# A two-layer hybrid mixer and MoE network on one core: the even layer's conditioning, gates and mLSTM moved between the outputs of its projection

## The reference, cut to what matters

```
mod = split(silu(c) @ ada_w[l] + ada_b[l], 6)          # for both layers; 0 shift, 1 scale, 2 gate of the mixer, 3..5 of the MoE
u = h * (1 + mod[1]) + mod[0]
p = u @ even_w_in                                      # 8 groups of 512 columns, and 16 gate columns
mLSTM, per head and direction (forward, backward):
    b = cumsum(log_sigmoid(f)); m = running max;       # from the gate columns
    s = (q k^T) * exp(log_d - m);  h = (s v) / max(|sum s|, exp(-m))
y_a = head_norm(h_fwd + h_bwd) * sigmoid(o)
y_b = HGRN(q, i, f_fwd, f_bwd) normed * silu(g)
y = [y_a, y_b] @ even_w_out;  h = layer_norm(ALPHA * h + mod[2] * y)
```

## Time and profile before

| | us |
|---|---|
| median of 3 runs (2417.41 to 2431.5) | 2421.47 |
| the profiled execution, its own time | 2445.92 |
| its span | 2444.1 |
| PE busy / DVE busy / ACT busy / POOL busy in the span | 1965.7 / 848.3 / 236.9 / 648.3 |
| mean granted TensorE clock | 0.892 |

### The profile page before, as it was taken

The page is one execution under the profiler, slowest core; times in us unless marked ns, Lnnn a source line. Parts: engine busy times, 40 slices in busy tenths (PEclk is TensorE's granted clock), DMA queues, the critical chain, the costliest instruction groups (busy, mean ns, idle before and its releaser), DMA issues. The chain is left out here.

```text
span 2444.1 us, 31822 instructions
## 1 busy us (share of the span) xinstructions
PE 1965.7 (80%) x10720; PEld 1014.9 (42%) x10721; DVE 848.3 (35%) x1752; ACT 236.9 (10%) x517; POOL 648.3 (27%) x935
## 2 busy tenths in 40 slices
PE   4795759945767998899999976859777988787795
PEld 0342523323445454455555433324454544344342
DVE  0004630068546232232332254644353222222224
ACT  1102110122020000000000011011110000000001
POOL 0000000000002555466565400000005554444440
PEclk8895679977887999899999987979878999999998
DMA  9400047300216899999899476130248999999944
GB/s 386 175 1 1 0 176 295 117 1 1 91 46 255 330 410 412 415 392 361 347 393 383 179 309 234 52 137 35 91 164 334 416 420 422 422 422 420 419 193 189
DMA packets 99975, 601.67 MB, mean 246 GB/s; under 512 B 23200, under 2 KB 23435, under 8 KB 40444
## 3 DMA queue, kind: packets, MB, share of 16 engines
q1 hardware_dynamic: 66012, 516.78, 51.7%
q0 software_dynamic: 33888, 83.86, 9.2%
HBM read 590.50 MB, written 51.92 MB: 263 GB/s over the span
## 5 line engine op out<-in xcount | busy, mean ns | idle before, releaser
L1600 PE MATMUL bank<-moe_w,blk_xT 128*64 128x256 f32 x5632 | 678.8, 396 | 2.7 <-issue 2.7
L1600 PEld LDWEIGHTS bank<-moe_w,blk_xT 128*64 128x64 f32 x5632 | 404.2, 142 | 220.0 <-issue 32.7
L1611 PE MATMUL bank<-moe_w,xt 128*64 128x512 f32 x1408 | 332.1, 592 | 1.5 <-DVE xt L1688 1.5
L1527 POOL DMA_INDIRECT ada_rows<-v_tokens,blk_gidx x264 | 272.5, 1032 | 140.0 <-issue 134.9
L1676 DVE STREAM_TRANSPOSE blk_xT<-ada_rows 128x512 f32<-128x512 f32 x132 | 93.9, 711 | 526.7 <-PE bank L1600 497.9
L451 PE MATMUL bank<-w_in_ring,xt 128*128 128x512 f32 x544 | 244.0, 609 | 12.6 <-DMA w_in_ring<-in_odd_w_in 9.7
L1543 POOL DMA_INDIRECT y_rows<-xt,blk_sidx x176 | 179.9, 1022 | 92.4 <-issue 55.0
L451 PEld LDWEIGHTS bank<-w_in_ring,xt 128*128 128x128 f32 x544 | 105.1, 195 | 148.7 <-issue 138.6
L1611 PEld LDWEIGHTS bank<-moe_w,xt 128*64 128x64 f32 x1408 | 100.9, 137 | 127.5 <-issue 100.5
L1659 ACT ACTIVATE xt<-bank 128x128 f32<-128x128 f32 x174 | 48.4, 278 | 1062.5 <-PE bank L1600 1062.5
L1695 DVE COPY xt<-bank 128x512 f32<-128x512 f32 x176 | 121.4, 690 | 75.0 <-PE bank L1611 73.2
(11 more groups left out here) (385 smaller groups left out, 1690.8 us busy)
## 6 DMA issues: line engine op xcount, KB each, us to landing
moe_w<-in_experts SPq DMA_DIRECT2D x128, 3072.0 KB
ada_ring<-in_ada_w SPq DMA_DIRECT2D x12, 2048.0 KB, 16.8
w_out<-in_ada_w POOLq DMA_DIRECT2D x12, 2048.0 KB, 8.2
moe_w<-y_rows SPq DMA_DIRECT2D x24, 1024.0 KB, 19.8
w_in_ring<-in_even_w_in SPq DMA_DIRECT2D x8, 2048.0 KB, 12.7
w_in_ring<-in_odd_w_in SPq DMA_DIRECT2D x7, 2048.0 KB, 20.9
ada_rows<-v_tokens,blk_gidx POOLq DMA_INDIRECT x264
w_out<-in_even_w_out SPq DMA_DIRECT2D x1, 4096.0 KB, 12.6
```

Source lines behind the costliest of these rows:

```text
L1527: pool.indirect_dma_start(came[q][:, u], None, v_quarters, bass.IndirectOffsetOnAxis(ap=gidx[q][:, u:u + 1], axis=0), bounds_check=4 * n_t ...
L1600: last = nc.tensor.matmul(g.bank[1][64 * h:64 * h + 64, 0:HID], xT[:, k], w[:, s, (2 * k + h) * HID:(2 * k + h + 1) * HID], start=k == 0, ...
L1611: last = nc.tensor.matmul(g.bank[3][64 * h:64 * h + 64, :], hT[:, 64 * m:64 * m + 64], w[:, s, at:at + 512], start=m == 0, stop=m == 1)
```

## The change

The stages 1 to 8 of the list above become three.

- `start_stage`: SP loads `c_cols`, then the four pieces of group 0 of layer 0 alone (shift and scale of the mixer), then the tables, the biases of both layers, and the tokens last. PE, ACT and DVE work the one group to its columns.
- `modulate_stage` without the gate rows (`rows` is None), with the loads of two groups of `even_w_in`; the ring has two places in place of three. The gate rows move to the start of `norm_stage` "h" (`mod_rows` on PE, four copies on ACT).
- `projection_stage` over all eight groups, 32 outputs, with `EvenSide` as its side. Two banks are left for the outputs (`BANKS = 2`; it was eight and six). The side has the other six: one for conditioning, one for the running maximum and the transposes of `mix`, two for scores (two key tiles at a time, so the scores are made in two halves), two for values. One more slot (`TAIL`) follows the last output.

What stands in the slots: gate columns in slot 1, their ACT and DVE parts in slots 2 to 4, their transposes in slot 6. Conditioning: five groups (the two others of layer 0, three of layer 1), a piece in each of four slots and the turn in the fifth, from slot 2. Heads: from slot 8, five slots per head; the last steps of a head (backward values, division, norm, transposes) stand in the slots of the next one, and those of the last head in slots 28 to 32. The head norm works on one head (128 x 512) at a time. POOL issues the loads of gate weights, tables and the 20 pieces, into a ring of two. Group 7 comes before group 6. Forward forget gates of the HGRN lie in `mix[:, 4:8]`. The stage `ada_columns_stage` of layer 1 is gone as well.

```
...
+    def load(self, eng):
+        for n, (i, l, group, part) in enumerate(self.pieces):
+            if n >= len(self.slots):
+                eng.wait_ge(self.used, n - len(self.slots) + 1)
...
+        if part == 0 and i:
+            pe.wait_ge(self.added, 2 * i)
...
+    def turn(self, pe, i):
+        pe.wait_ge(self.copied, 4 * (i + 1))
...
+def start_stage(g):
...
+                sp.dma_start(g.c_cols[:], g.dram["c_cols"]).then_inc(c_loaded, 16)
+                ada.load(sp)
+                sp.dma_start(g.base[:], g.dram["t_base"]).then_inc(table_loaded, 16)
+                sp.dma_start(g.ada_bias[:], g.dram["ada_b"].rearrange("l p c -> p l c")).then_inc(bias_loaded, 16)
+                sp.dma_start(g.h[:], g.dram["x_all"]).then_inc(h_loaded, 16)
+                sp.wait_ge(h_loaded, 16)
...
+                pe.wait_ge(act_done, 1)
+                for n in range(len(ada.pieces)):
+                    ada.multiply(pe, n)
+                pe.wait_ge(table_loaded, 16)
+                ada.turn(pe, 0)
...
 def modulate_stage(g, l, shift, scale, tiles, rows, prefetch):
...
-            for v in range(2):
-                for k in range(KT):
-                    col = mods[:, rows * KT + k, v:v + 1].broadcast_to([P, P])
-                    last = nc.tensor.matmul(g.bank[4 + 2 * v + k // 4][:, (k % 4) * P:(k % 4 + 1) * P], col, g.ident,
-                                            start=True, stop=True)
...
+            if rows is not None:
+                mod_rows(g, l, rows).then_inc(row_ready, 1)
...
+            if rows is None:
+                return
...
-        BANKS = 6 if side else 8
+        BANKS = side.BANKS if side else 8
+        slots = len(outs) + (side.TAIL if side else 0)
...
+class EvenSide:
...
+    BANKS, TAIL = 2, 1
+    ADA_BANK, ROW_BANK, SCORE_BANKS, VALUE_BANKS = 2, 3, (4, 5), (6, 7)
+    GATE_BANK = 4
+    ADA_STEPS = (2, 7, 12, 17, 22)
+    HEAD0, PER_HEAD = 8, 5
...
+        pool.dma_start(self.wg[:], self.g.dram["w_gates"]).then_inc(self.loaded, 16)
+        pool.dma_start(self.gb[:], self.g.dram["gate_b"]).then_inc(self.loaded, 16)
+        pool.dma_start(self.negsel[:], self.g.dram["t_negsel"].rearrange("h (a b) -> h a b", a=HEADS)).then_inc(self.side_loaded, 16)
+        pool.dma_start(self.w, self.g.dram["mlstm_norm_w"]).then_inc(self.side_loaded, 16)
+        self.ada.load(pool)
...
+    def pe(self, pe, n):
...
+        if n == 1:
+            pe.wait_ge(self.loaded, 32)
...
+        if n == 6:
+            pe.wait_ge(self.step, self.n_rows)
...
+        for i, at in enumerate(self.ADA_STEPS):
+            if at <= n < at + 4:
+                self.ada.multiply(pe, 4 * i + n - at)
+            if n == at + 4:
+                self.ada.turn(pe, i)
+        h, a = self.head_step(n)
+        if a == 0 and h < HEADS:
+            self.max_row(pe, h, 0)
+            self.scores(pe, h, 0)
+        if a == 1:
+            if h < HEADS:
+                self.max_row(pe, h, 1)
+            if h >= 1:
+                self.values(pe, h - 1, 1)
+        if a == 3 and h < HEADS:
+            self.scores(pe, h, 1)
+        if a == 4:
+            if h < HEADS:
+                self.values(pe, h, 0)
+            if h >= 1:
+                self.turn_mix(pe, h - 1)
+    def max_row(self, pe, h, d):
+        if h == 0 and d == 0:
+            pe.wait_ge(self.side_loaded, 32)
+        elif d == 0:
+            pe.wait_ge(self.clamped, self.through(h - 1, 1))
+            if h >= 2:
+                pe.wait_ge(self.mix_copied, h - 1)
+        else:
+            pe.wait_ge(self.clamped, self.through(h, 0))
...
+    def scores(self, pe, h, jj):
+        s = self.s
+        if jj:
+            pe.wait_ge(self.weighted, self.weighed(h, 1, 0))
+        elif h:
+            pe.wait_ge(self.weighted, self.weighed(h - 1, 1, 1))
+        else:
+            pe.wait_ge(self.activated, 3)
...
+    def values(self, pe, h, d):
+        pe.wait_ge(self.weighted, self.weighed(h, d, 1))
+        if h or d:
+            pe.wait_ge(self.read, 2 * h + d)
...
+    def turn_mix(self, pe, h):
+        pe.wait_ge(self.normed, h + 1)
+        if h + 1 < HEADS:
+            pe.wait_ge(self.clamped, self.through(h + 1, 1))
...
+    def act(self, act, n):
...
+        if n == 2:
+            act.wait_ge(self.made, 1)
...
+        if n == 3:
+            act.wait_ge(self.step, self.n_abs)
...
+        if n == 7:
+            act.wait_ge(self.turned, 1)
...
+            if n == at + 3:
+                self.ada.copy(act, i)
...
+        if a in (0, 1) and h < HEADS:
+            for m, (j, k, x, y) in enumerate(self.pieces[a]):
...
+        if a == 3 and h >= 1:
+            act.wait_ge(self.var_ready, h)
...
+        if a == 4 and h >= 1:
+            act.wait_ge(self.mix_turned, h)
...
+    def dve(self, dve, n):
...
+        if n == 2:
+            dve.wait_ge(self.loaded, 32)
...
+        if n == 4:
+            dve.wait_ge(self.activated, 1)
...
+            if n == at + 4:
+                self.ada.add(dve, i)
...
+        if a == 0:
+            if own:
+                self.clamp(dve, h, 0)
+            if old:
+                self.finish(dve, h - 1, 0)
+        if a == 1 and own:
+            self.weigh(dve, h, 0, 0)
+            self.clamp(dve, h, 1)
+        if a == 2:
+            if own:
+                self.weigh(dve, h, 1, 0)
+            if old:
+                self.finish(dve, h - 1, 1)
+                self.norm_sums(h - 1)
+        if a == 3:
+            if own:
+                self.weigh(dve, h, 0, 1)
+            if old:
+                self.norm_scale(dve, h - 1)
+        if a == 4 and own:
+            self.weigh(dve, h, 1, 1)
...
 def even_layer(g):
     nc = g.nc
-    ada_columns_stage(g, 0)
...
+        ff = g.mix[:, 4:8]
...
-            gates_wrapped(g, s)
-            mlstm_stage(g, s)
-            norm_stage(g, y[:], allt, HEADS, True, o[:], "mlstm_norm_w", 0, "m")
...
+            w_in = InputWeights(g, c3, g.dram["even_w_in"], [0, 1, 2, 3, 4, 5, 7, 6], 2)
+            modulate_stage(g, 0, 0, 1, allt, None, w_in)
...
             projection_stage(g, g.dram["even_w_in"], [
+                (0, "T", allt, lambda j: (qT if j < 2 else kT)[:, j % 2], "q_scale"),
+                (1, "N", allt, lambda j: v1[:, j, :, 0:P], "heads"),
+                (2, "N", allt, lambda j: o[:, j], "sigmoid"),
                 (3, "T", allt, lambda j: q[:, j], "silu"),
                 (4, "N", allt, lambda j: v[:, j], "copy"),
                 (5, "T", allt, lambda j: ff[:, j], "sigmoid"),
-                (6, "T", allt, lambda j: fb[:, j], "sigmoid"),
-                (7, "N", allt, lambda j: hg[:, j], "silu")], lambda _: AdaRows(g, 1, work, 2, (6, 7)))
-            ada_columns_stage(g, 1)
-            hgrn_stage(g, work, {"q": q[:], "v": v, "f": (ff[:], fb[:]), "y": y})
-            norm_stage(g, y[:], allt, HEADS, False, hg[:], "hgrn_norm_w", 4, "h", w_out)
+                (7, "N", allt, lambda j: hg[:, j], "silu"),
+                (6, "T", allt, lambda j: fb[:, j], "sigmoid")],
+                lambda ctx: EvenSide(g, ctx, s, room, [late[:, i] for i in range(2)]), prefetched=w_in)
+        w_out = Prefetch(g, ctx, "w_out0", [P, KT, D], g.dram["even_w_out"])
+        work = w_out.tile[:].rearrange("p k d -> p (k d)")
+        y = sb("h_y", [P, HEADS, T])
+        hgrn_stage(g, work, {"q": q[:], "v": v, "f": (ff, fb), "y": y})
+        norm_stage(g, y[:], allt, HEADS, False, hg, "hgrn_norm_w", 4, "h", w_out, (0, 2))
...
```

More of the change, by code:

```diff
@@ L275, in _ @@
             def _(sp):
[L276 removed]
+                sp.dma_start(g.c_cols[:], g.dram["c_cols"]).then_inc(c_loaded, 16)
[4 more added lines that the diff above has]
+                sp.wait_ge(h_loaded, 16)
+            @block.gpsimd
@@ L318, in _, with mod_rows @@
-                for which in (1, 4):
-                    part = mods[:, which * KT:(which + 1) * KT, :]
-                    link(nc.vector.tensor_scalar(part, part, 1.0, None, ALU.add))
+                ada.add(dve, 0)
+def mod_rows(g, l, which):
+    for v in range(2):
+        for k in range(KT):
+            col = g.mods[:, l, which * KT + k, v:v + 1].broadcast_to([P, P])
+            last = g.nc.tensor.matmul(g.bank[4 + 2 * v + k // 4][:, (k % 4) * P:(k % 4 + 1) * P], col, g.ident,
+                                      start=True, stop=True)
+    return last
@@ L721, in norm_stage @@
+def norm_stage(g, y, tiles, groups, center, gate, w_name, mix_base, tag, prefetch=None, rows=None):
     nc = g.nc
```

559 lines of the change are left out of this document (252 added, 307 removed).

## The result

| | before | after |
|---|---|---|
| median of 4 runs each | 2420.89 us (2417.41 to 2431.5) | 2297.19 us (2290.13 to 2300.33) |
| ratio, 95% interval | | 0.9478 [0.9447, 0.9509] |
| profiled execution, its span | 2445.9, 2444.1 us | 2297.83, 2296.0 us |
| PE, DVE, ACT busy | 1965.7 (80%), 848.3, 236.9 us | 1926.3 (84%), 854.0, 261.1 us |
| start of the projection | 94.5 us | 41.2 us |

Forecast 2291, measured 2297. The stretches of the kernel after that answer to the earlier trace rows: the conditioning at the start, the modulation, the one stage, the middle of it, and the norm of the HGRN. The columns are those of the earlier trace rows.

What follows compares the result with a forecast made beforehand. Bound: chains between engines that leave PE idle or slow, to be laid beside the projection's matmuls. Saved 53.4 (start) + 79.9 (stage) − 2.5 (norm) = 130.8, so 2421.5 − 130.8 = 2291 us; range 2276 to 2318.

Steps and rivals of the forecast that it cites:

- The start: Opening up to the first projection matmul: start moves from 94.5 to 41.1 us, saving 53.4, bounds 51 to 56.
- just there: End of the start: the projection's first group of weights needs 7.9 us and lands just as the projection starts.
- The stage: Merged projection stage: if PE never waits, its work sums to 332.2 us in place of 412.1, saving 79.9.
- its sign: Merged stage: 325 to 340 us long, clock near 1.00, PE busy over 97%, if the prediction is right.
- values: Term of the merged stage's sum for the mLSTM values on PE: eight times 3.57 us, 28.6.
- Why PE doesn't wait: Merged stage: results are asked for a whole output later, at least 6.87 us, so no PE step waits.
- Rival 1: Merged stage: the slots hold PE up, 48 us of waits come back, 2339 us; chance 0.15.
- its 28 steps: PE steps waiting for DVE or ACT: eight maxima, eight score halves, eight values, four turns; 1.7 us each.
- Rival 2: Merged stage: short mLSTM matmuls draw the clock down for the outputs too, 194 us in all, 2485; chance 0.05.
- The norm: HGRN's norm with the gate rows: root at about 7.5 us instead of 4.9, 2.5 lost, 0 to 4.
- The subtraction from the median: Saving worked out on the 2445.9 us profiled execution, 130.8, taken unchanged from the median: 2421.5 to 2291.
- The inner range: Whole kernel: the forecast's own range from the bounds of its terms, 2279 to 2303 us.

Runs made afterwards that it cites:

- Run 9: Changed kernel with the tables, biases and residual issued ahead of the four conditioning pieces in the opening block: 2312.75 us, ratio 0.9492.
- the copy: The kernel before, unedited, measured and traced a second time: 2421.26 us, ratio 0.9993.
- runs 3 to 6: Changed kernel with all heads behind the outputs (2368.49 us), one output bank (2300.58), ten more DVE squares a head (2295.43), thirty more (2353.13).
- run 3: Changed kernel with all four heads behind the last output, not between outputs: 2368.49 us, ratio 0.9777.
- the three traces of before: Kernel before as first profiled (span 2444.1 us), unedited again (2419.0), and with an unused tile of 384 bytes a partition (2425.7).
- the two copies: Second, unedited runs of both kernels: the kernel before 2421.26 us, the changed kernel 2294.83 us.

## Why the prediction was right

**The start.** Predicted 41.1, measured 41.17. By parts: first use 9.06 (9.1), fourth 23.65 (24.1), modulation 32.18 (32.2). The weights of the projection were "just there", as predicted. The list puts PE's 2.8 us ahead of L431 down to them, but PE had to wait for ACT in any case: before, the same place shows 2.84 us without a wait for weights, and ACT ends `xt` at 33.30 + 7.39 = 40.69, 0.48 ahead of the first matmul. Run 9 confirms that the arrival of the pieces is what counts.

**The stage.** It is what the prediction said, a sum of PE work with nothing between: no wait, clock 1.00, 316.67 of 318 us busy. The sum was 14.6 us too long, 332.2 against 317.6, so the stage fell short of its sign (325 to 340 us), and the HGRN started at 358.8, not at 370 to 380. The terms, each measured from its start to the start of what follows:

| term | predicted | measured |
|---|---|---|
| 32 outputs and the cold start | 219.8 + 2.0 = 221.8 | 225.4 (the first 8.55, the others 6.87 to 7.07) |
| 20 pieces | 40.4 | 36.6 (1.83 each) |
| gate columns | 7.2 | 7.0 |
| maxima | 9.0 | 8 × 1.05 = 8.4 |
| scores | 14.8 | 8 × 1.91 = 15.3 |
| values | 28.6 | 6 × 2.34 + 2 × 2.23 = 18.5 |
| transposes | 8.8 | 5.4 |
| tail | 1.6 | 1.1 |

The 32 outputs are 256 matmuls, so 512 PE instructions. The kernel before has them in two projections: 12 outputs (96 matmuls, 192 instructions) ahead of the mLSTM and 20 behind it.

The groups of short PE instructions behind the table (busy us, mean ns, and idle before):

```profile
L624 PE MATMUL bank<-m_v,mlstm_e 128*128 128x129 f32 x160 | 19.8, 279 | 0.0
L614 PE MATMUL bank<-m_qT,m_kT 64*128 64x512 f32 x32 | 15.8, 615 | 0.0
...
L232 PE MATMUL bank<-base,ada_rows 128*128 128x128 f32 x20 | 3.1, 275 | 0.0
L634 PE MATMUL bank<-base,mlstm_y 128*128 128x128 f32 x16 | 2.4, 272 | 0.0
L568 PE MATMUL bank<-base,mix 4*128 4x4 f32 x16 | 1.1, 199 | 0.0
```

The mis-sized term is the values, 10.1 us. I took 3.57 us from a row in a stage whose mean clock was 0.59 as if it were a price at the upper level, while I halved the scores from the same stage for just that reason. 20 PE instructions of 129 columns take 2.34 at the upper level. A second trace of the kernel before would have shown it, in the copy's mLSTM:

```profile
237.29 2.50 PE L635 MATMUL bank<-m_v,mlstm_e 128*128 128x129 f32 x20
```

**Why PE doesn't wait.** Argued from the order of slots alone, and shown by runs 3 to 6: one bank costs 3 us of waits, 6.9 us more DVE a head cost next to nothing, and the heads wait when no outputs stand between them or when DVE gets 20.8 us more a head. Rival 1 (48 us of waits) is refuted: of its 28 steps none waits. The 1.7 us a step that the rival took from the mLSTM of before were paid where PE had nothing else to do.

**The clock.** Rival 2 (2485) is refuted by the 1.00 of the stage and, with one bank, by 0.99. The Trainium skill ("TensorE: Matmul & The Clock Gate", section "A second HAM failure mode: psum-queue depth-cycling") expects trouble from cycling through banks with small idles between groups; no run here shows it, since PE has no idles to speak of with two banks or with one. That fewer banks would be worse was the prediction's own step. Where PE does idle, in the heads of run 3, the clock is 0.64.

**The norm.** Predicted 2.5, measured 7.2 − 4.9 = 2.3. The whole HGRN segment can't tell it: it takes 130.0 to 137.1 us in the three traces of before. PE's waits in it are the same to 0.3 us in all three; what differs is how long the same 689 or so PE instructions take, 53.25, 55.94 and 60.48 us in segments of 130.0, 132.7 and 137.1 us, at a mean clock of 0.72, 0.70 and 0.68.

**The subtraction from the median.** The gain was made against the profiled execution, and the 24 us above the median were set aside as untouched by the change. This step failed, without consequence: 10.6 of them lay in the very stages that were replaced, whose rows did not run "at even, repeated durations", so from the copy of before the stage saves 83.7, not 94.5. The balance of the two copies: start −55.1, stage −83.7, MoE 1 +10.5, HGRN −4.3, the rest +3.6, together −129.0, the difference of the spans 2419.0 and 2290.0. The forecast was −130.8, with the start and the stage 5.5 too small for such a run, 2.5 lost in the HGRN where its scatter gave 4.3 back, and MoE 1 missing altogether. That the forecast came within 6 us of the median is in part luck: the 14.6 too many in the stage's sum met 10.6 too many in the profiled execution that it was subtracted from, and the placement term, which it did not have, is worth more than the 6 us.

**The range.** The inner range, 2279 to 2303, does not follow from the bounds that it names: with 30 us for short matmuls at the lower level alone the high end would be above 2320. It is rather the forecast and 12 us to either side.

## What to carry to other kernels

Short chains between engines cost next to nothing here once each step was separated from the next by a piece of long matmul work, and as long as the slot could carry the chain's own work (6.9 us more of DVE a head fitted, 20.8 did not). So first find the stage whose engine is full, lay the chains into its gaps by a slot or more, then price the stage as a sum of its own instructions, at the clock level it will run at and not at that of the stage from which the row comes. When any tile is added, ask which streams land in tiles that move: pad to the old alignment, and compare untouched stages of both traces. Before subtracting from a median what was worked out on one profiled execution, find where that execution was longer.
